# A transformer layer pair on one core: the first stage and the opening of the delta-rule scan in another order

## The reference, cut to what matters

```
h = modulate(rms_norm(x, g), shift, scale)        # h * (1 + scale) + shift, other shift and scale for context and latent
p = h @ w_in                                      # 256 context tokens and 256 latent tokens
qkv = silu(depthwise_conv(p[:, :3 * 1024]))
q, k, v = split(qkv); q = l2_normalize(q); k = l2_normalize(k)      # per head of 128
decay = exp(where(incl, g_i - g_j, -inf))
m = where(strict, (k * beta) @ k^T * decay, 0); attn = (q @ k^T) * decay
```

## Time and profile before

| | |
|---|---|
| median of 3 runs | 2140.53 us (2136.24 to 2142.3) |
| the profiled execution | 2144.49 us |
| its span | 2142.5 us |
| TensorE busy | 1928.8 us (90%) |
| VectorE, ScalarE, GpSimd busy | 620.3, 436.5, 67.3 us |
| granted TensorE clock, mean | 0.971 |

### The profile page before, as it was taken

One profiled execution on the slowest core, in us unless ns is written; L12 is line 12 of the kernel. 1 busy time (PEld: TensorE's weight loads), 2 busy tenths in 40 slices (PEclk: granted clock), 3 DMA queues, 4 the chain that ended last, 5 costly groups with the idle time before them and its releaser, 6 DMA issues. The chain is left out here.

```text
span 2142.5 us, 24885 instructions
## 1 busy us (share of the span) xinstructions
PE 1928.8 (90%) x9335; PEld 1043.1 (49%) x9336; DVE 620.3 (29%) x1355; ACT 436.5 (20%) x865; POOL 67.3 (3%) x86
## 2 busy tenths in 40 slices
PE   5999797899989889999988889899988889999997
PEld 2436354887878543333333332333333244767775
DVE  2476347246520211111111111111111122433223
ACT  2122550327221011111111100111111021620111
POOL 1000310100000000000000000000000000000000
PEclk9999898799999989999999999999999989999999
DMA  9443336315464459999999999999999961214442
GB/s 353 148 167 139 132 99 141 102 52 173 136 220 172 189 235 418 419 418 417 417 417 417 417 418 419 419 418 417 417 418 417 412 241 70 111 50 147 147 156 108
DMA packets 150939, 566.73 MB, mean 265 GB/s; under 512 B 35904, under 2 KB 43840, under 8 KB 113024
## 3 DMA queue, kind: packets, MB, share of 16 engines
q1 hardware_dynamic: 150880, 565.92, 68.2%
HBM read 555.26 MB, written 10.62 MB: 264 GB/s over the span
## 5 line engine op out<-in xcount | busy, mean ns | idle before, releaser
L2021 PE MATMUL expert_gb<-expert_ring,hT 128*64 128x512 f32 x1024 | 270.6, 607 | 70.1 <-DMA expert_ring<-in_w_gu 68.6
L2021 PE MATMUL expert_lb<-expert_ring,hT 128*64 128x512 f32 x1024 | 262.8, 592 | 0.0
L1926 DVE TENSOR_SCALAR hT<-expert_gb 128x512 f32<-128x512 f32 x32 | 22.1, 692 | 717.9 <-PE expert_lb L2021 717.9
L2069 PE MATMUL expert_yb<-expert_ring,hT 128*64 128x512 f32 x512 | 222.7, 592 | 1.5 <-DMA expert_ring<-in_w_down 1.4
L2069 PE MATMUL expert_yb<-expert_ring,h2T 128*64 128x512 f32 x512 | 222.8, 592 | 0.0
L2021 PEld LDWEIGHTS expert_gb<-expert_ring,hT 128*64 128x64 f32 x1024 | 59.2, 135 | 251.3 <-DMA expert_ring<-in_w_gu 202.5
L453 PE MATMUL mix_in_pj<-hT,mix_in_pj_ring 128*128 128x512 f32 (+1 forms) x384 | 144.0, 533 | 3.8 <-DVE hT L574 3.8
L2021 PEld LDWEIGHTS expert_lb<-expert_ring,hT 128*64 128x64 f32 x1024 | 72.8, 137 | 146.9 <-issue 146.9
L2419 PE MATMUL attend_bank<-hT,expert_ring 128*128 128x256 f32 x640 | 141.4, 379 | 0.0
L2069 PEld LDWEIGHTS expert_yb<-expert_ring,hT 128*64 128x64 f32 x512 | 69.9, 137 | 143.2 <-issue 140.4
L2419 PEld LDWEIGHTS attend_bank<-hT,expert_ring 128*128 128x128 f32 x640 | 121.6, 190 | 25.1 <-issue 9.6
(11 more groups left out here) (469 smaller groups left out, 2285.8 us busy)
## 6 DMA issues: line engine op xcount, KB each, us to landing
expert_ring<-in_w_gu SPq DMA_DIRECT2D x256, 1024.0 KB, 19.7
expert_ring<-in_w_down SPq DMA_DIRECT2D x128, 1024.0 KB, 20.7
fill_w<-in_w_fill SPq DMA_DIRECT2D x48, 512.0 KB, 3.7
mix_in_wm<-in_w_mod SPq DMA_DIRECT2D x11, 2048.0 KB, 9.1
expert_ring<-in_w_up_units SPq DMA_DIRECT2D x22, 1024.0 KB, 5.7
mix_in_pj_ring<-in_w_in_units SPq DMA_DIRECT2D x12, 1024.0 KB, 4.8
expert_ring<-in_w_down SPq DMA_DIRECT2D x22, 512.0 KB, 3.4
expert_ring<-in_w_in SPq DMA_DIRECT2D x4, 2048.0 KB, 11.6
```

What stands on the lines that cost most here:

```text
L1926: v.tensor_scalar(glu, gb[j][:], LIMIT, None, ALU.min).then_inc(s_glu, 1)
L2021: m = pe.matmul(b[halves[h], :], xT[:, k, x], ring[:, z, c0 + 512 * h:c0 + 512 * h + 512], start=False, stop=(k == KT - 1))
L2069: m = pe.matmul(yb[h][halves[j], :], hidT[j][:, c, hh * SLOTS:(hh + 1) * SLOTS], ring[:, z, a * F + 512 * h:a * F + 512 * h + 512], start= ...
```

## The change

1. The affine step is divided: VectorE does the eight latent halves, ScalarE the eight context halves (`ACT.Identity` with scale and bias), each with a semaphore of its own, and `project(0)` waits for both.
2. The SiLUs of k, v and q move from the start of the scan to the end of the first stage on ScalarE: k and v once the taps of unit 7 are done, with the copy of fill 0 between them, q once the last taps are done.
3. SP's store of the bias parts moves ahead of the stores of the rows.
4. In the scan `decay(0)` comes behind the roots of k, the eight `Ln` of k stand together ahead of the two `Exp`; GpSimd squares q before it waits for the masks' tables; VectorE scales q behind the products of tile 0; the waits for the SiLUs go.
5. `w_mod` lies in memory by units, so that a partition's 8 x 512 numbers of a unit are one run of 16 KB. It was 8 runs of 2 KB.

```
+                sp.wait_ge(s_bs, 7)
+                sp.dma_start(A.bias_split.rearrange("n p c -> p n c"), parts[:]).then_inc(s_o, 16)
                 sp.wait_ge(s_v, ENDS_AT)
                 sp.wait_ge(s_a, 4)
...
                     S.fill.load(sp, f + 2)
-                sp.wait_ge(s_bs, 7)
-                sp.dma_start(A.bias_split.rearrange("n p c -> p n c"), parts[:]).then_inc(s_o, 16)
                 sp.wait_ge(s_o, 112)
...
                 mod_row(3)
+                act.wait_ge(s_xt, 2 * NTILE)
+                act.wait_ge(s_ab, 3)
+                for k in range(KT):
+                    act.activation(S.hT[:, k, 0:L], S.hT[:, k, 0:L], ACT.Identity, scale=a1[:, 1, k:k + 1],
+                                   bias=mcol[:, k, 1:2]).then_inc(s_hc, 1)
...
-                for f, b in enumerate((small, pc)):
-                    S.fill.copy(act, f, b)
+                act.wait_ge(s_k, TAPS_DONE[7])
+                for c in (slice(0, HA), slice(HA, 2 * HA)):
+                    for g in range(2):
+                        x8 = S.pkv[:, c.start + 4 * g:c.start + 4 * g + 4]
+                        act.activation(x8, x8, ACT.Silu)
+                    if c.start == 0:
+                        S.fill.copy(act, 0, small)
+                act.wait_ge(s_k, TAPS_DONE[NPJ - 1])
+                act.activation(S.pq[:], S.pq[:], ACT.Silu)
+                S.fill.copy(act, 1, pc)
...
-                                pe.wait_ge(s_ht, 2 * (k + 1))
+                                pe.wait_ge(s_ht, k + 1)
+                                pe.wait_ge(s_hc, k + 1)
...
-                    for q in range(2):
-                        c = slice(L, 2 * L) if q == 0 else slice(0, L)
-                        v.tensor_scalar(S.hT[:, k, c], S.hT[:, k, c], a1[:, q, k:k + 1], mcol[:, k, q:q + 1],
-                                        ALU.mult, ALU.add).then_inc(s_ht, 1)
+                    v.tensor_scalar(S.hT[:, k, L:2 * L], S.hT[:, k, L:2 * L], a1[:, 0, k:k + 1], mcol[:, k, 0:1],
+                                    ALU.mult, ALU.add).then_inc(s_ht, 1)
...
+                copy_fill(2)
+                for h in range(HA):
+                    see(act, ("kn", h))
+                    act.activation(sq[:, h, :], flat(TURN["kn", h][0]), ACT.Ln, bias=C.eps[:]).then_inc(freesem(("kn", h)), 1)
                 for g in g2:
-                    act.activation(k[:, heads[g]], k[:, heads[g]], ACT.Silu).then_inc(s_sk, 1)
-                for g in g2:
-                    act.activation(v_[:, heads[g]], v_[:, heads[g]], ACT.Silu).then_inc(s_sv, 1)
-                act.activation(q[:], q[:], ACT.Silu).then_inc(s_qs, 1)
-                copy_fill(2)
-                decay(0)
...
+                decay(0)
                 copy_fill(3)
...
-                mask(0)
-                g.wait_ge(s_qs, 1)
-                g.tensor_tensor(sqq, q[:], q[:], ALU.mult).then_inc(s_sqq, 1)
-                for t in range(1, NTILE):
+                for t in range(NTILE):
                     mask(t)
...
-        "w_mod": f(x["w_mod"][0]),
+        "w_mod_units": f(x["w_mod"][0].reshape(KT, P, -1, 512).transpose(2, 1, 0, 3)),
```

More of the change, by code:

```diff
@@ L215, in mix_in_stage @@
         s_col, s_ss, s_rv, s_rs, s_xn = s.sem("columns"), s.sem("squares"), s.sem("mean_square"), s.sem("rstd"), s.sem("xn")
-        s_tr, s_xt, s_ab, s_ht = s.sem("x_turned"), s.sem("x_copied"), s.sem("affine"), s.sem("hT_done")
+        s_tr, s_xt, s_ab, s_ht, s_hc = s.sem("x_turned"), s.sem("x_copied"), s.sem("affine"), s.sem("hT_latent"), s.sem("hT_context")
         s_pw, s_pf, s_pe, s_k = s.sems("pj_in", 2), s.sems("pj_full", 2), s.sems("pj_copied", 2), s.sem("taps")
@@ L267, in later @@
                     see_pm(sp, f"u{n - 2 if n >= HEAD + 2 else z}")
-                    sp.dma_start(wm[:, z], A.w_mod[:, n * 512:(n + 1) * 512].rearrange("(k p) n -> p k n", p=P)).then_inc(s_w2[z], 16)
+                    sp.dma_start(wm[:, z], A.w_mod_units[n]).then_inc(s_w2[z], 16)
                 sp.dma_start(ccol[:], A.ccol).then_inc(s_cc, 16)
                 for n in range(HEAD):
-                    sp.dma_start(wm[:, n] if n < HEAD - 1 else first, A.w_mod[:, n * 512:(n + 1) * 512].rearrange("(k p) n -> p k n", p=P)).then_inc(s_w[n], 16)
+                    sp.dma_start(wm[:, n] if n < HEAD - 1 else first, A.w_mod_units[n]).then_inc(s_w[n], 16)
                     if n == 0:
@@ L474, in _ @@
                 pe.wait_ge(s_sw, 16)
-                pe.wait_ge(s_ht, 2 * KT)
+                pe.wait_ge(s_ht, KT)
+                pe.wait_ge(s_hc, KT)
                 for k in range(KT):
@@ L733, in delta_scan_stage @@
         s_in, s_row = s.sem("tables_in"), s.sems("rows_in", 2)
-        s_sk, s_sv, s_qs, s_sqk, s_sqq = (s.sem(n) for n in ("k_silu", "v_silu", "q_silu", "k_squared", "q_squared"))
+        s_sqk, s_sqq = s.sem("k_squared"), s.sem("q_squared")
         s_ln, s_rtk, s_rtq, s_nk, s_nq = (s.sem(n) for n in ("logs", "k_roots", "q_roots", "k_normed", "q_normed"))
@@ L827, in decay @@
                         m.then_inc(s_dm[d], 1)
+                copy_fill(2)
+                for h in range(HA):
+                    see(act, ("kn", h))
+                    act.activation(sq[:, h, :], flat(TURN["kn", h][0]), ACT.Ln, bias=C.eps[:]).then_inc(freesem(("kn", h)), 1)
                 for g in g2:
-                    act.activation(k[:, heads[g]], k[:, heads[g]], ACT.Silu).then_inc(s_sk, 1)
-                for g in g2:
-                    act.activation(v_[:, heads[g]], v_[:, heads[g]], ACT.Silu).then_inc(s_sv, 1)
-                act.activation(q[:], q[:], ACT.Silu).then_inc(s_qs, 1)
-                copy_fill(2)
-                decay(0)
-                for g in g2:
-                    for h in range(HALF * g, HALF * g + HALF):
-                        see(act, ("kn", h))
-                        act.activation(sq[:, h, :], flat(TURN["kn", h][0]), ACT.Ln, bias=C.eps[:]).then_inc(freesem(("kn", h)), 1)
                     copied(act, ("kn", HALF * g + HALF - 1))
                     act.activation(sq[:, heads[g]], sq[:, heads[g]], ACT.Exp, scale=-0.5).then_inc(s_rtk, 1)
+                decay(0)
                 copy_fill(3)
@@ L906, in _ @@
                 g.memset(xx[1], 0.0).then_inc(s_x0, 1)
+                g.tensor_tensor(sqq, q[:], q[:], ALU.mult).then_inc(s_sqq, 1)
                 g.wait_ge(s_x0, 1)
@@ L927, in _ @@
                 for g in g2:
-                    v.wait_ge(s_sk, g + 1)
                     v.tensor_tensor(sq[:, heads[g]], k[:, heads[g]], k[:, heads[g]], ALU.mult).then_inc(s_sqk, 1)
@@ L936, in _ @@
                     v.tensor_tensor(k[:, heads[g]], k[:, heads[g]], sq[:, heads[g]], ALU.mult).then_inc(s_nk, 1)
-                v.wait_ge(s_rtq, 1)
-                v.scalar_tensor_tensor(q[:], q[:], DK, sqq, ALU.mult, ALU.mult).then_inc(s_nq, 1)
                 for t in range(NTILE):
+                    if t == 1:
+                        v.wait_ge(s_rtq, 1)
+                        v.scalar_tensor_tensor(q[:], q[:], DK, sqq, ALU.mult, ALU.mult).then_inc(s_nq, 1)
                     for d in d2:
@@ L1042, in _ @@
                 fill(2)
-                pe.wait_ge(s_sv, 2)
                 for t in range(NTILE):
```

## The result

| | before | after |
|---|---|---|
| median of the runs taken together | 2140.58 us (2136.24 to 2142.3) | 2122.27 us (2120.16 to 2125.23) |
| the profiled execution, its span | 2144.49, 2142.5 us | 2120.16, 2118.1 us |
| granted TensorE clock, mean | 0.971 | 0.976 |

The ratio after to before is 0.9915, 95% interval 0.9898 to 0.9931: 18.3 us less by the medians, where 18.6 were forecast. The forecast of 2121.9 us was right.

A forecast was written before the change was run, and what follows sets the result against it. Four hold-ups on the path ahead of 305 us were taken to bound it. Gains of 1.6 + 4.5 + 5.4 + 7.1 = 18.6 us off 2144.5 give 2125.9; the runs' median lies 4.0 lower: 2121.9 us, range 2116 to 2128.5.

The forecast's parts named there:

- the end of the last product group: VectorE's last product group in the scan, 304.3 us before; forecast near 285.6, with gains ahead of it staying won.
- Rows of `w_mod`: Head: four units ahead of the columns load 0.40 us faster each with longer rows, 1.6 us gained (0 to 2.1).
- the ring's 418: GB/s of the projection ring with 8 KB per partition, taken as the rate for the longer `w_mod` rows, against 387.
- Affine step: First two projections: with the step on two engines TensorE's waits go, 4.5 us gained (2.4 to 6.2).
- the 1.7 us kept for it: First projections: one of TensorE's two half-clock stretches was assumed to stay, costing 1.7 us.
- the second, at 50 us behind the waits, I let go: First projections: TensorE's second half-clock stretch, behind the waits at 50 us, was assumed to vanish with them.
- The rival of the clock: TensorE falls to half clock twice anyway: affine gains 2.4, `w_mod` rows 0, 14.9 us in all, 2125.6; chance 0.11.
- Bias store: End of first stage: SP's list ends 0.45 + 5.0 us sooner, 5.4 us gained (5.0 to 6.9).
- SiLUs: End of first stage: ScalarE finishes them at 228.1, wanted at 228.92; cost 0, with 0.8 us to spare.
- Opening: Scan's start to tile 2's products: TensorE's order bounds, 54.5 us become 47.4, 7.1 us gained (4 to 7.6).
- The sum of 47.4 us: Scan's opening: TensorE's fills, v, `kn`, `qn` and products of tiles 0 and 1 added up without idle time.
- The rule on table loads: ScalarE: the skill page's 1.38 us drain per table switch would cut the gain from 18.6 to 14.8 us; not adopted.

The follow-up runs named there:

- u_affine_pool: Changed kernel with the affine step on VectorE alone and GpSimd starting the bias parts only after it; 2121.88 us.
- after_again: The changed kernel run and profiled once more, unedited; 2122.5 us, ratio to before 0.9903.
- u_order: Changed kernel with the old order of the scan's opening, SiLUs still early; 2132.75 us, ratio to before 0.9967.
- best: Changed kernel with two unused products ahead of `project(0)` and fill 5 moved behind the turning of k; 2118.74 us, ratio to before 0.99.
- warm: Changed kernel with two unused 128x512 products on TensorE between the columns and `project(0)`; 2122.34 us.

## Why the prediction was right, point by point

**What bounds the kernel.** The prediction took one moment, the end of the last product group, as the measure of everything ahead of it. That held: 18.86 us less there, 18.63 at the first matmul behind the substitution, 17.84 at the start of the next stage.

**Rows of `w_mod`: 1.6 forecast, 1.9 measured** between the means, with ends of 0 and 2.1. The rate was taken a little low: 16 KB rows ran at 422 to 442 GB/s in nine profiles, and at 406 in one, where the ring's 418 had been reckoned. The upper end said that TensorE's own order would bound from there. That is so in three profiles of ten, where the wait for unit 3 is gone; in the other seven a wait of 0.15 to 0.89 us is left.

**Affine step: 4.5 forecast, 3.64 measured in place, 1.4 to 2.0 by the pieces in the whole, and none that the medians show.** The waits inside `project(0)` went, and one stretch at low clock remained. It was longer than the 1.7 us kept for it: 6.8 us from about 35, of which some 5 us lie within the projection, worth 2.5, and `project(0)` with `project(1)` took 30.35 us where 28.0 + 1.7 were reckoned. ScalarE's instruction took 586 ns, and the eight 4.04 us, 0.5 each, not the 0.33 to 0.42 us that came from a plain copy: an ACTIVATE with scale and bias from columns was priced by one without. It did no harm, since TensorE takes about 0.88 us per block. And the division of the work was not what the gain needed: sixteen instructions on VectorE do as well once GpSimd is quiet (u_affine_pool). What failed is the step "the second, at 50 us behind the waits, I let go": that stretch did go, but another one came behind the second columns at 161 us. The rival of the clock had the right mechanism, and looked for it in the wrong place.

**Bias store: 5.4 forecast, 5.42 measured in the gap**, and fill 2 was 1.44 us shorter besides, in the profile after; with after_again's 10.13 us, none of that can be counted on, and it was left out rightly. What failed is that the term was costed by itself. Taken from the changed kernel it is worth 6.0 us by the medians, added to the old one 0.4 (1.5 by the ratio, 3.4 at most). The prediction said that GpSimd's masks start when their tables land, and used it for the new order only. In the old order `decay(0)` stands ahead of the roots of k, so the tables' landing sets the time there, and it came only 2.8 us sooner (248.01 for 250.80) when the stage began 4.7 us sooner. That explains some 2 of the missing us; the rest is the single profile's time behind the scan.

**SiLUs: cost 0 forecast, 0.88 us of slack measured** where 0.8 had been worked out. Their gain was inside the 7.1 of the opening: alone it is 1.56 us there, so the rest is the order's.

**Opening: 7.1 forecast.** Fill 2 to last group went from 67.24 to 57.87 us, 9.37 less, of which 1.44 is fill 2's clock: 7.9. The upper end was 7.6. The sum of 47.4 us added the groups' durations as they stand in the rows, but each group begins before the last one's duration is over: a fill takes 7.03 us in its row and the next group starts 6.87 us behind its start. Over `kn` and the fills this makes some 0.8 us. `kn` without a gap, no wait of VectorE for ScalarE at its product groups, and `decay(3)` 2.5 us ahead of need (2.3 had been reckoned). One cost had been left out: VectorE's squares of k took 7.90 us in place of about 4.5, since GpSimd's square of q now runs beside them; they ended at 235.35, and `kn` needed them at 238.04 only. In u_order, where only GpSimd's two MEMSETs run beside them, they take the old time:

```profile
228.89 4.49 DVE L935 TENSOR_TENSOR delta_scan_ktok<-pkv 128x2048 f32<-128x2048 f32 x2 [9.33 <-PEq L78]
```

**The sum.** That it came within 0.4 us is in part luck. In the profile after, the affine step brought 1.95 us (3.64 less the 1.69 lost near 161 us) where 4.5 were forecast, and rows and opening brought 2.8 more than forecast, 1.44 of it from the clock in fill 2. It also took all parts together. The parts taken away one at a time from the changed kernel (rows, affine, store, SiLUs, order) are worth 3.1, 0.2, 6.0, 0.9 and 10.5 us by the medians against its 2122.27, together 20.7; only store and order stand clear of the spread. Added one at a time to the old kernel, the store gives 0.4 by the median (1.5 by the ratio) and the order 8.7 (7.9).

**The rule on table loads.** With 1.38 us more at each load ScalarE would have been 3.2 us late at `decay(3)` and 0.6 at the stage's end; it was 2.5 and 0.88 us early. ScalarE after, a load with its next instruction 0.02 us behind it:

```profile
245.81 1.28 ACT L848 ACT_TABLE_LOAD   x1
247.11 3.71 ACT L848 ACTIVATE delta_scan_ktok<-delta_scan_ktok 128x2048 f32<-128x2048 f32 x2
```

The drain that the Trainium skill (ScalarE: Activation LUTs, What ACT_TABLE_LOAD costs) adds is not in these rows; where the page and the trace differ, the trace was right to go by.

## What to carry to other kernels

Before a wait is priced by its length, ask what would be late next in the order of the other engines: a store's 5 us were worth 6 ahead of one order of instructions and 0 to 3 ahead of another, and the row that told part of it (masks waiting for a table's DMA) was in the profile of before. An engine that is slow in a step may be slow because of its neighbour: let the neighbour wait first, and divide the work only if that doesn't do. A few us won on TensorE at one place can be lost at another 120 us later, when a stretch at low clock appears there, so compare pieces of the timeline and medians, and not one landmark of one profile.

## What the runs showed of the hardware

- VectorE beside GpSimd. The same 128x256 TENSOR_SCALAR took 407 ns alone and up to 2032 ns beside GpSimd's work on the biases; sixteen took 5.26 us alone and 11.16 beside it. In "best", where the affine step came 1.2 us later than in the profile after, eight instructions took 5.32 us in place of 2.67, because GpSimd started within them (at 38.45). ScalarE's eight in the profile after, the last of them with GpSimd at work from 38.38 on, stayed at 585 to 599 ns each.
- The granted clock of TensorE falls from 1.00 to 0.50 (1.2 GHz) while the columns run or just behind them, 32 matmuls that are two columns wide, in every profile of the study at 33 to 39 us, and at the second columns at 159 to 162 us in nine of fourteen. The stretches lasted 3.4 us or a multiple of it. They came or stayed away between two executions of one program (54.5 and 75.0 us in all within the first 480). What decides it in a single execution was not found, and full-width products behind the columns (warm) did not prevent it. Fill 2 came out at 7.1 us in seven of the eleven profiles in which TensorE had been idle 2.8 us ahead of it, and at 8.5 to 10.1 us in the other four and in all three with 8.2 us of idling or more.
- An ACTIVATE with Identity, scale and bias from columns takes 585 to 600 ns for 128x256, in after and after_again, and eight in a row take 4.04 us; the plain copy of the same shape out of PSUM takes 381 ns in the profile before, and two in a row 0.66 us.
